# A streaming-encoder layer in one kernel: score offsets by rounded products, merged columns one chunk later, the last expert in halves, one unit of transfers in the columns' buffer

## The reference, cut to what matters

```python
h = rmsnorm(x, g_mix)
proj = h @ w_in                     # q, k, v, pool, z, xbc, dt, three gates of 1024
# differential attention, 4 heads, per head two maps m of 64 columns, causal by blocks of 64
s = einsum('bqhmd,bkhmd->bhmqk', qblk, k)
s = s + bias[None, :, None]         # bias = rel_table[rel_bucket(kpos - qpos)], by head
p = softmax(where(visible, s, -inf))
attn = p[:, :, 0] - lam * p[:, :, 1]
o_a = rmsnorm(attn @ v, subln_g)
o_b = pool_mixer(...); o_c = ssd_mixer(...)
merged = sum_b sigmoid(gate_b) * (o_b @ w_branch[b])
x = x + merged @ w_mix_out
x = x + cross_attention(rmsnorm(x), rmsnorm(mem))      # 4 heads, 256 memory rows
h = rmsnorm(x, g_moe)                                   # router: best group, its best 2 of 4 experts
for e in range(16):
    y = y + comb[:, e:e+1] * ((silu(h @ w_gate[e]) * (h @ w_up[e])) @ w_down[e])
out = rmsnorm(x + y, g_final)
```

## Time and profile before

| | |
|---|---|
| median of 3 runs | 513.97 us (513.95 to 514.27) |
| the profiled execution | 513.97 us |
| its span on the core | 512.2 us |
| TensorE busy | 492.1 us, 96% |
| VectorE busy | 247.9 us, 48% |
| ScalarE busy | 195.6 us, 38% |
| GpSimd busy | 15.7 us, 3% |
| transfers | 149.28 MB, mean 291 GB/s |
| mean granted clock of TensorE | 0.992 |

### The profile page before, as it was taken

The page is one execution under the profiler, slowest core; times in us unless marked ns, Lnnn a source line. Parts: engine busy times, 40 slices in busy tenths (PEclk is TensorE's granted clock), DMA queues, the critical chain, the costliest instruction groups (busy, mean ns, idle before and its releaser), DMA issues.

```text
span 512.2 us, 7124 instructions
## 1 busy us (share of the span) xinstructions
PE 492.1 (96%) x2772; PEld 333.9 (65%) x2772; DVE 247.9 (48%) x469; ACT 195.6 (38%) x349; POOL 15.7 (3%) x30
## 2 busy tenths in 40 slices
PE   7999999999999999999999899999999999999982
PEld 7998998778888988788998534433443344433330
DVE  3764599876788689985664621111111111111113
ACT  5454757446726455445674201111211121111113
POOL 2000100000030000000100000000000000000000
PEclk9999999999999999999999899999999999999998
DMA  7797647643544548896769999999999999999992
GB/s 252 260 312 200 216 132 226 194 117 119 160 162 153 197 125 279 277 355 199 268 230 371 405 401 394 400 399 402 404 402 399 401 400 404 404 399 399 400 357 87
DMA packets 68026, 149.28 MB, mean 291 GB/s; under 512 B 8790, under 2 KB 15124, under 8 KB 67988
## 3 DMA queue, kind: packets, MB, share of 16 engines
q1 hardware_dynamic: 67684, 148.24, 80.5%
q10 hardware_dynamic: 304, 0.53, 0.3%
HBM read 147.69 MB, written 1.05 MB: 290 GB/s over the span
## 4 chain that ended last, share of the span: by engine, by line
issue 47%; PE 34%; DVE 14%; ACT 2%; DMA 1%; POOL 0%; SPq 0%; POOLq 0%; DVEq 0%; ACTq 0%
PE bank L1422 9%; PE bank L1424 9%; PE bank L1423 9%; DVE wl L930 6%; DMA raw<-in_w_in 1%; DVE gates L1189 1%; DVE xc L946 1%; ACT wh L570 1%; PE bank L1445 1%; PE bank L1532 1%; DVE gates L1192 1%; PE bank L1555 1%; DVE big L976 1%; DVE al L916 1%; DVE al L923 1%
## 5 line engine op out<-in xcount | busy, mean ns | idle before, releaser
L930 DVE TENSOR_TENSOR wl<-raw,wh 128x1024 fp32r<-128x1024 f32 (+1 forms) x80 | 94.2, 1195 | 35.2 <-ACT wh L570 33.7
L570 ACT ACTIVATE wh<-raw 128x1024 fp32r<-128x1024 f32 (+1 forms) x80 | 81.9, 1043 | 67.5 <-PE bank L1424 50.8
L1422 PE MATMUL bank<-wh,ah 128*128 128x512 f32 (+2 forms) x248 | 95.0, 383 | 0.0
L1423 PE MATMUL bank<-wl,ah 128*128 128x512 f32 (+2 forms) x248 | 93.3, 376 | 0.0
L1424 PE MATMUL bank<-wh,al 128*128 128x512 f32 (+2 forms) x248 | 93.3, 376 | 0.0
L1424 PEld LDWEIGHTS bank<-wh,al 128*128 128x128 f32 x248 | 46.6, 188 | 8.6
L1422 PEld LDWEIGHTS bank<-wh,ah 128*128 128x128 f32 x248 | 46.7, 188 | 8.3 <-issue 0.3
L1423 PEld LDWEIGHTS bank<-wl,ah 128*128 128x128 f32 x248 | 46.7, 188 | 7.8
L1422 PE MATMUL bank<-ah,wh 128*128 128x256 f32 x160 | 45.8, 286 | 2.2 <-DVE al L916 1.2
L1423 PE MATMUL bank<-al,wh 128*128 128x256 f32 x160 | 45.3, 283 | 0.0
L1424 PE MATMUL bank<-ah,wl 128*128 128x256 f32 x160 | 45.2, 283 | 0.0
(11 more groups left out here) (352 smaller groups left out, 900.1 us busy)
## 6 DMA issues: line engine op xcount, KB each, us to landing
raw<-in_w_in SPq DMA_DIRECT2D x48, 512.0 KB, 4.7
wh_raw<-in_w_exp_up SPq DMA_DIRECT2D x14, 512.0 KB, 12.4
wl_raw<-in_w_exp_gate SPq DMA_DIRECT2D x13, 512.0 KB, 11.2
gates<-in_w_exp_down SPq DMA_DIRECT2D x13, 512.0 KB, 13.3
raw<-in_w_branch SPq DMA_DIRECT2D x12, 512.0 KB, 4.1
ah_raw<-in_w_exp_up SPq DMA_DIRECT2D x10, 512.0 KB, 12.2
al_raw<-in_w_exp_gate SPq DMA_DIRECT2D x10, 512.0 KB, 11.4
gates<-in_w_exp_gate SPq DMA_DIRECT2D x9, 512.0 KB, 11.5
```

The source lines that it names most:

```text
L570: act.activation(dst, src, ACT.Copy, scale=scale).then_inc(done, 1)
L930: dve.tensor_tensor(wl[:, n % RING, 0:sz], raw[:, n % RING, 0:sz], wh[:, n % RING, 0:sz].bitcast(F32), ALU.subtract)\
L1422: pe.matmul(dst, st[0], mv[0], start=start, stop=False, skip_group_check=True)
L1423: pe.matmul(dst, st[0], mv[1], start=False, stop=False, skip_group_check=True)
```

## The change

Six edits stand in one diff.

*Offsets.* The table `toep` is split once into two rounded parts, `bias_hi` (ScalarE, at `n` = `FIRST["bcd"] + 1`, which is behind the cast of chunk 16) and `bias_lo` (VectorE, one `n` later), both [128, 4, 384]: the 256 columns of the second block of queries and again the 128 of the first. The mirror matrix is copied once to the rounded type, `flip_r`. `scores` adds the offsets with four rounded products of 384 columns instead of four float32 ones of 256 and 128. GpSimd's memset of the table's corner comes earlier in its program. The three buffers lie over parts of `gates`.

*Slots.* In slot `s`, `scores(s)` comes ahead of `attn_T(s-1)`.

*Merged columns.* The halves of `to_cols("mix")` come at `LAST["b21"]` and `FIRST["m0"]` instead of `FIRST["b21"]` and `LAST["mka"]`.

*Mean.* The squares are scaled by `D ** -0.5`, and one VectorE instruction makes the mean with its epsilon instead of two.

*Router.* Eleven dummy products ahead of the ranks instead of three; VectorE makes the second half of the gathered rows after `select(0)`; the first gather does the products with the high parts first.

*Last expert and one unit.* The unit of expert 2 that holds the fourth pair of gate and up chunks (`SOLO`) is loaded once into the buffer of the merged columns, `al0`, outside the ring; the other units close up. The last expert's down product, its scaling, subtraction and scatter are done in two halves of 256 columns each, in banks of their own.

```diff
-FILLS = [len(range(s, PASS, RAWX // 2)) for s in range(RAWX // 2)]
+SOLO = UNIT["gu", 2, 3]
+ORDER = [u for u in range(PASS) if u != SOLO]
+FILLS = [len(range(s, len(ORDER), RAWX // 2)) for s in range(RAWX // 2)]
...
-WARM = (10, 6, 5, 6, 0, 0, 4, 3)
+WARM = (10, 6, 5, 6, 0, 0, 4, 11)
...
+        bias_hi, bias_lo = (over_("gates", f"bias_{part}", [P, HEADS, 384], F32R, skip=4 * at)
+                            for part, at in (("hi", 3 * 512), ("lo", 3 * D + 2 * 512)))
+        flip_r = over_("gates", "flip_r", [P, P], F32R, skip=4 * (3 * 512 - P))
...
+        al0_raw = over_("al0", "al0_raw", [P, 2, CH])
+        SOLO_AT = next(j for j, (_, freed) in enumerate(HOMES) if freed == "logits")
+        SOLO_SLOT = len(HOMES) // 2
+        HOMES += [(al0_raw[:, j, :], "values") for j in range(2)]
         FIN_SLOT = RAWG
         g_fin = HOMES[FIN_SLOT][0]
         def fast_fill(u):
-            return u % (RAWX // 2), u // (RAWX // 2) + 1
+            if u == SOLO:
+                return SOLO_SLOT, 1
+            at = ORDER.index(u)
+            return at % (RAWX // 2), at // (RAWX // 2) + 1
+        def landed(slot, times):
+            if slot == SOLO_SLOT:
+                return arrived[0], 16 * len(range(0, CHUNKS, RAW)) + 32
...
-            for c in range(EARLY, 2 * PASS):
-                slot = c % RAWX
-                if c < RAWX:
+            chunks = [2 * u + j for u in ORDER for j in range(2)]
+            for at in range(EARLY, len(chunks)):
+                c, slot = chunks[at], at % RAWX
+                if at == SOLO_AT:
+                    sp.wait_ge(used, LAST["mv"] + 1)
+                    for j in range(2):
+                        load_chunk(2 * SOLO_SLOT + j, 2 * SOLO + j, UNITS)
+                if at < RAWX:
                     free_by = HOMES[slot][1]
                     if free_by == "mixed":
                         sp.wait_ge(s_("cols_pe"), COLS["mix"] + 4)
...
+            g.wait_ge(s_("toep_in"), 16 * HEADS)
+            g.memset(toep[64:P, :, S - SEEN:S], LOW).then_inc(s_("toep_ready"), 1)
             for t in range(T):
                 norm_rstd("mem", t, mem_rs, mem_ss)
-            g.wait_ge(s_("rstd"), NORM["mem"] + T)
-            g.wait_ge(s_("toep_in"), 16 * HEADS)
-            g.memset(toep[64:P, :, S - SEEN:S], LOW).then_inc(s_("toep_ready"), 1)
...
+                if n == FIRST["bcd"] + 1:
+                    act.wait_ge(s_("consts_set"), 1)
+                    act.activation(flip_r[:, :], flip[:, :], ACT.Copy).then_inc(s_("toep_ready"), 1)
+                    act.wait_ge(s_("toep_ready"), 2)
+                    hi_of(bias_hi[:, :, 0:256], toep[:, :, :], s_("toep_ready"))
+                    hi_of(bias_hi[:, :, 256:384], toep[:, :, P:S], s_("toep_ready"))
...
+            def y_last_hi():
+                for j, c in enumerate(COL_HALF):
+                    if j:
+                        act.wait_ge(spent, PASS)
+                    else:
+                        act.wait_ge(filled, len(NAMES) + 1)
+                    act.activation(yh_last[:, c], y_last_bank[j][:, 0:256], ACT.Copy, scale=combs[:, 1:2]).then_inc(s_("y_hi"), 1)
...
-                link(dve.tensor_tensor(ss, ss4[:, 0:2], ss4[:, 2:4], ALU.add))
-                dve.tensor_scalar(ss, ss, 1.0 / D, EPS, ALU.mult, ALU.add).then_inc(s_("x_mean_square"), 1)
+                dve.scalar_tensor_tensor(out=ss, in0=ss4[:, 0:2], scalar=EPS, in1=ss4[:, 2:4], op0=ALU.add, op1=ALU.add)\
+                    .then_inc(s_("x_mean_square"), 1)
...
+                if n == FIRST["bcd"] + 2:
+                    dve.wait_ge(s_("toep_ready"), 4)
+                    for at, lo in ((0, 0), (256, P)):
+                        dve.tensor_tensor(bias_lo[:, :, at:at + S - lo], toep[:, :, lo:S], bias_hi[:, :, at:at + S - lo].bitcast(F32),
+                                          ALU.subtract).then_inc(s_("toep_ready"), 1)
...
-            for t in range(T):
-                moe_rows(t, 0, D // 2)
+            moe_rows(0, 0, D // 2)
...
             link(dve.tensor_tensor(key[:, :, :], bank[1][:, 0:T * EXPERTS].rearrange("p (t n) -> p t n", t=T), chosen, ALU.mult))
             select(0)
+            moe_rows(1, 0, D // 2)
             dve.tensor_copy(totals, bank[1][:, T * EXPERTS:(T + 1) * EXPERTS]).then_inc(s_("totals_ready"), 1)
...
-                    last = n == EXPERTS + 1
-                    y_lo(yl_last if last else yl, yh_last if last else yh, p, ybank(n - 2), n - 1)
+                if 2 <= n <= EXPERTS:
+                    y_lo(yl[:, :], yh[:, :], p, bank[1][:, :], n - 1)
+                if n == EXPERTS + 1:
+                    for j, c in enumerate(COL_HALF):
+                        y_lo(yl_last[:, c], yh_last[:, c], p, y_last_bank[j][:, 0:256], EXPERTS + j)
             with dve.If(over > 0):
...
                     pe.wait_ge(s_("score_exp"), 4 * h)
-                blocks = [(t, w, lo, m, dst[:, 256 * (1 - t):256 * (1 - t) + w])
-                          for t, w, lo in ((1, 256, 0), (0, 128, 128)) for m, dst in enumerate((pS1, pS0))]
-                for t, w, _, m, d in blocks:
+                blocks = [(t, w, m, dst[:, 256 * (1 - t):256 * (1 - t) + w])
+                          for t, w in ((1, 256), (0, 128)) for m, dst in enumerate((pS1, pS0))]
+                for t, w, m, d in blocks:
                     pe.matmul(d, qT[QK * m:QK * m + QK, h, P * t:P * t + P], kT[QK * m:QK * m + QK, h, 0:w],
                               start=(t == 1), stop=False, skip_group_check=True)
-                for t, w, lo, _, d in blocks:
-                    mm = pe.matmul(d, flip[:, :], toep[:, h, lo:lo + w], start=False, stop=True, skip_group_check=True)
+                for dst in (pS1, pS0):
+                    for part in (bias_hi, bias_lo):
+                        mm = pe.matmul(dst[:, 0:384], flip_r[:, :], part[:, h, :], start=False, stop=part is bias_lo, skip_group_check=True)
                 mm.then_inc(s_("scores_pe"), 1)
...
                 if s == 0:
-                    pe.wait_ge(s_("toep_ready"), 1)
...
                         for half in range(2):
                             pe.wait_ge(free[2 * (NAMES.index(nm) % 2) + half], NAMES.index(nm) // 2 + 1)
                 if 2 <= s < 6:
                     attn_o(s - 2)
+                if 0 <= s < 4:
+                    scores(s)
                 if 1 <= s < 5:
                     attn_T(s - 1)
-                if 0 <= s < 4:
...
                     to_cols("mem", hm, s_("mem_rows"), 2, KD, (pS1, pS0, pT, pO), 2)
-                if n in (FIRST["b21"], LAST["mka"]):
-                    half = int(n == LAST["mka"])
+                if n in (LAST["b21"], FIRST["m0"]):
...
+            keep_warm(WARM[7], bank[2])
...
-            pe.wait_ge(s_("sel_ready"), 1)
-            pe.wait_ge(s_("moe_rows"), T)
-            gather(0, 0, bank[3])
+            def down_last(j, fill):
+                slot, times = fill
+                pe.wait_ge(*landed(slot, times))
+                w = [HOMES[2 * slot + i][0].rearrange("p (k n) -> p k n", k=2) for i in range(2)]
+                for c, dst in zip(COL_HALF, y_last_bank):
+                    for kk in range(2):
+                        kt = 2 * j + kk
+                        for i in range(2):
+                            mm = pe.matmul(dst[row_half[i], 0:256], aT[:, kt, row_half[i]], w[i][:, kk, c], start=(kt == 0), stop=(kt == 3),
+                                           skip_group_check=True)
+                    if j and c is COL_HALF[0]:
+                        mm.then_inc(filled, 1)
+                mm.then_inc(spent, 1)
+            def scatter_last():
+                for j, c in enumerate(COL_HALF):
+                    pe.wait_ge(s_("y_lo"), EXPERTS + j)
+                    for t in range(T):
+                        for part in (yh_last, yl_last):
+                            mm = pe.matmul(bank[5 + 2 * t][:, c], selT[:, 1, t, :], part[:, c], start=False, stop=True, skip_group_check=True)
+                        if j:
+                            mm.then_inc(s_("scatter_pe"), 1)
+            def first_gather():
+                pe.wait_ge(s_("sel_ready"), 1)
+                pe.wait_ge(s_("rows_hi"), T)
+                for rows in (rows_hi, rows_lo):
+                    if rows is rows_lo:
+                        pe.wait_ge(s_("moe_rows"), T)
+                    for t in range(T):
+                        for kt in range(2):
+                            mm = pe.matmul(bank[3][:, 256 * kt:256 * kt + 256], rows[:, t, 0:256].rearrange("a (p k) -> a k p", k=2)[:, kt, :],
+                                           sel[:, 0, t, :], start=(rows is rows_hi and t == 0 and kt == 0), stop=(rows is rows_lo and t == T - 1),
+                                           skip_group_check=True)
+                mm.then_inc(s_("gather_pe"), 1)
...
-                    scatter(k // 2, k % 2, (yh_last, yl_last) if k == EXPERTS - 1 else (yh, yl))
+                    scatter(k // 2, k % 2)
```

(7 more changed lines are left out.)

54 lines of the change are left out of this document (29 added, 25 removed).

## The result

The changed kernel takes 515.16 us in the median of 9 runs (514.53 to 516.39), the kernel before 513.97 in 9 runs (513.49 to 515.31). The ratio is 1.0021, 95% interval 1.0012 to 1.0031. The interval leaves 1 out, so the change costs about 1.1 us; that is the very edge of what I had called distinguishable from no change (0.2%). The forecast was 514.2, the range 512.3 to 515.7. Of the four cases the number of the third (515.3) came out, though not by its mechanism.

A forecast was written before the change was run, and what follows sets the result against it. Bounds, stage by stage: the ScalarE-VectorE-TensorE hand-over without slack, VectorE in the slots, TensorE to 183 us, transfers from 290 to 480, then a serial tail. 513.97 + 2.7 − 1.4 − 0.2 − 0.86 = 514.2 us; range 512.3 to 515.7.

The forecast's parts named there:

- the third: The case of Rival 3: slower by the preparation itself or the `x` slots' pause, 515.3 us; chance 0.15.
- Preparation: Rounding the offsets on ScalarE and VectorE makes chunk `pool` 1 start late: +2.7 us, bounds 1.2 and 3.8.
- none of the three hand-overs above has slack: Around 50 to 68 us ScalarE, VectorE and TensorE pass the delay on in full, so `pool` 1 starts 2.7 us late.
- Slots: Attention slots: VectorE is the slower engine; earlier scores remove its 0.72 us wait, plus 0.7 at the last transpose: -1.4 us.
- Merged columns: Products one chunk later: the 0.82 us wait at 216.91 goes, TensorE waits ahead of `m0` until 223.5: -0.2 us, bounds 0 and -0.82.
- Transfers: Ranks, first gather, extra unit: first expert 0.5 us earlier, but transfers bound what follows: 0, up to +1.1 if not covered.
- Tail: Last expert in halves and merged mean, behind the last landing: -0.86 us, bounds -0.4 and -1.4.
- Rival 1: The offsets' preparation is hidden in idle time: 512.2 us taken, 512.7 with 1.2 us left, 511.5 with nothing; chance 0.2.
- Rival 2: TensorE's clock falls behind waits near 71 and 131 us, costing 1.7 us of work: 515.9 us; chance 0.1.
- its dear half: The clock fall of Rival 2 near 131 us, behind the last attention transpose, where nothing hides the 1.7 us.
- Rival 3: Preparation costs 3.8 instead of 2.7 us (four-block accesses half again as dear), or the `x` slots' pause: 515.3 us; chance 0.15.

The follow-up runs named there:

- experiment 1: The changed kernel without the rounded offsets: no preparation on ScalarE and VectorE, float32 offset products of before, all else kept; 513.43 us, ratio 0.9981 to the kernel before.
- experiment 7: The changed kernel with the same offsets prepared earlier, at `LAST["v"]`: ScalarE two chunks earlier, VectorE three; 512.72 us, ratio 0.9967 to the kernel before.
- experiment 2: The changed kernel with the roundings and subtractions of the offsets on GpSimd instead of ScalarE and VectorE; 513.97 us, ratio 0.9993 to the kernel before.
- experiment 12: Early offsets, merged-column products at their old places, no dummies ahead of the ranks, no unit in the columns' buffer (old transfer order); 511.74 us, ratio 0.9955.
- experiment 10: The kernel with the early offsets (experiment 7), without dummy products ahead of the ranks; 512.18 us, ratio 0.9962 to the kernel before.
- experiment 3: The changed kernel with three dummy products ahead of the ranks instead of eleven; 514.67 us, ratio 1.0004 to the kernel before.
- experiment 4: The changed kernel with 22 dummy products ahead of the ranks instead of eleven; 515.89 us, ratio 1.0042 to the kernel before.
- experiment 9: The kernel with the early offsets (experiment 7), with TensorE's products for the merged columns at their old places, one chunk earlier; 512.19 us, ratio 0.9958.

## Why the prediction came out as it did

The time fell into the range, and part of that was luck. Four lines of the ledger came out dearer than forecast (columns 0.30, transfers 0.52, up to the first store 0.41, the stores 0.43), 1.7 us together, and they alone would have given 515.9, above the range. The preparation was cheaper by 0.41 and the program started 0.35 earlier, which took 0.8 back.

**Preparation (+2.7; +2.29 in the trace).** The mechanism was right and is shown from both sides: experiment 1 takes the work away and experiment 7 moves it to idle time, and both bring `pool` 1 back to 56.0 us behind the first product. Up to the start of `dt_arg`'s exponential the arithmetic holds to a hundredth: 57.45 for 55.10 is 2.35 late, 2.70 without the early start of 0.35. The 0.4 that are missing at `pool` 1 are the part of the step that failed, "none of the three hand-overs above has slack": the cast of chunk 19, which follows, is only 2.44 late and that of chunk 20 2.33, so ScalarE had small gaps that my three rows didn't show. In the kernel before it is idle for 0.17 us ahead of chunk 19's cast, in the changed one not at all.

**Slots (-1.4; -1.39).** The sum was right, a reading under it was not. I had VectorE at work "without a gap, except for the 0.72". It also stands idle for 1.79 us in each of the four slots, waiting for ScalarE's exponentials, before (first two rows) and in the changed kernel (third):

```profile
101.26 0.18 DVE L1001 RECIPROCAL small<-small 128x4 f32<-128x4 f32 x1 [1.79 <-ACT pr L616]
110.19 0.18 DVE L1001 RECIPROCAL small<-small 128x4 f32<-128x4 f32 x1 [1.79 <-ACT pr L616]
...
112.14 0.18 DVE L1040 RECIPROCAL small<-small 128x4 f32<-128x4 f32 x1 [1.79 <-ACT pr L639]
```

So VectorE and ScalarE together, each waiting for the other in turn, set the pace of the slots. That TensorE does not is shown by the 1.3 us of low clock, which experiments 2 and 7 don't have and which make no difference at chunk 40. The wait for ScalarE's `ant` copy that I had named is there too, 1.02 us at 112.54. The split was not in the forecast: the two edits overlap (1.13 and 0.84 alone).

**Merged columns (-0.2; +0.10).** The wait that I had foreseen is there, and is longer:

```profile
224.25 0.47 PE L1467 MATMUL bank<-wh,ah 128*128 128x512 f32 x1 [1.12 <-DVEq L1234]
...
223.25 0.69 DVE L1233 SCALAR_TENSOR_TENSOR gates<-gates,bank 128x512 f32<-128x512 f32 x1
...
227.08 1.03 PE L1490 MATMUL bank<-ident,gates 128*128 128x128 f32 x8
```

I had the bank free at 223.5. TensorE started 0.75 later, of which 0.58 is what the whole trace is late there. VectorE's instruction ends at 223.94, which without these 0.58 is the 223.36 of my three rows. The step that failed is the guess of 0.1 for the hand-over to TensorE: it takes 0.31. So the move gains nothing, outside the bounds that I had given.

**Transfers (0; +0.52).** This is the term that failed by most. "The same bytes go over the queue" is true, and the share of 1.04 has not moved. Yet the last landing is later in every trace with the unit in the columns' buffer, and not without it (experiment 12). It does not need the `x` slots' longer pause, for which I had named a price of up to 1.1 (experiment 10). The other half of this term failed too: the first expert was to start 0.5 us earlier, and starts 15.67 us behind chunk 79 instead of 14.38, since the dummies cost more and gave no clock back. As I had it, the transfers hide that. The streams run level for most of the way: the landings 158 and 159 of 192 lie at 178.6 us behind chunk 79 (on average of the two) before and 178.4 changed, the landings 164 and 165 at 186.5 and 187.0, with 400 GB/s moved in both all the while. Counted in bytes they stay level to the end: by 220 us behind chunk 79 all transfers had moved 147.13 MB before, 147.15 changed and 147.06 in experiment 12. So it is not the amount moved that is late, but the completion of single transfers. What shifts it by half a microsecond at the same rate stays open; experiment 12 is one trace, and ties it to the order of the queue, not to a mechanism.

**Tail (-0.86; -0.45).** From the last unit's first product to the third square it is 3.64 us where I had 3.72 and the earlier trace rows gave 4.40. Two things took half of it back. The last unit starts 0.71 us behind its landing instead of 0.31, because the scatter of expert 14, which stands ahead of it, ended only then (its last product starts at 500.94); and the mean saved 0.09 of its 0.18:

```profile
501.26 0.43 PE L1888 MATMUL bank<-x,pr 128*64 128x256 f32 x1
...
503.75 0.60 ACT L902 ACTIVATE hm<-bank 128x512 f32<-128x512 f32 x1
504.90 0.60 ACT L902 ACTIVATE hm<-bank 128x512 f32<-128x512 f32 x1
505.48 0.60 ACT L902 ACTIVATE hm<-bank 128x512 f32<-128x512 f32 x1
...
504.54 1.89 DVE L1448 TENSOR_TENSOR hm<-bank,raw 128x512 f32<-128x512 f32 x3 [0.29 <-ACT hm L902]
506.35 0.15 DVE L948 SCALAR_TENSOR_TENSOR small<-small 128x2 f32<-128x2 f32 x1
```

ScalarE now does all four squares behind the two scalings; before, two of them lay in its wait. VectorE's gain products pile up behind them, and the mean starts at 506.35, when three of them are through. Whether the stores then give the 0.45 back (5.31 on average behind halves, 4.72 behind whole columns, with a scatter of 0.5) is not settled.

**The rivals.** Rival 1, the hidden preparation, did not happen where the change put it, and is what experiment 7 made: its ratio on 513.97 gives 512.3, where I had given 512.2 to 512.7. Rival 2: the clock fell behind the wait of 2.51 us at `pool` 1, to 0.71 over 71 to 75, and the slots' pace hid it. The Trainium skill ("TensorE: Matmul & The Clock Gate", section "HAM oscillation — how this bites in real kernels") says that a long enough wait for data sends the engine back to the lower clock. This trace agrees, and experiment 2, with a wait of 1.01 us at the same place, stays at 1.00. Ahead of the last transposes TensorE waited 0.26 us, not 1, and the clock there stayed at 1.00, so its dear half did not come. The dummies ahead of the ranks did not keep the clock, which is 0.93 over 266 to 290 as before: it fell ahead of them. Rival 3: the preparation in its four-block shape cost what the plain shapes cost (1.58 and 1.82 us), not half again as much; its 515.3 is near the result for other reasons.

## What to carry to other kernels

Work that is added to an engine costs what the hand-over behind it has no slack for, whatever the engine's share says: follow the chunks in flight from engine to engine and look for the place where each has idle time behind its own instruction. The same three roundings and two subtractions cost 2.3 us at one `n` and nothing two to three chunks earlier. An engine that shows idle time can still set the pace, when it and another wait for each other in turn, as VectorE and ScalarE do in the slots. Two edits that take away the same wait don't add up, so test each alone before both are kept.

When the transfers bound the end, compare when the last one lands, not how busy the queue is.

## What the runs showed of the hardware that I had not expected

GpSimd's subtraction and VectorE's did not run side by side: VectorE's took 2.20 instead of 0.71 us and 2.32 instead of 1.23 beside GpSimd's, and 1.21 behind them (experiment 2).

The granted clock of TensorE also fell where the engine had not waited. In the changed kernel it is busy in 4.00 of 4.00 us in the stretches 268 to 272, 272 to 276 and 276 to 280, each at 1.00; then six rows of float32 products with 512 columns take 4.52 us instead of the 2.82 of the first trace before:

```profile
280.81 4.52 PE L1779 MATMUL bank<-x,ident 128*128 128x512 f32 x6
285.17 2.62 PE L1474 MATMUL bank<-ident 128*128 128x128 f32 x22
```

What ran just before were 32 rows of products with 20 columns, with four 128x128 transposes among them. It is so, at 4.34 to 5.47 us, in nine of the fourteen traces, the second one of the kernel before among them, while the first had its fall behind the wait of 1.29 us at 284.25. In the other four (experiments 2, 3, 4 and 9) the clock stays at 1.00 there, though the same products run. The dummies come behind it and neither cause nor prevent it: it falls with none and with eleven, and stays with 3, 11 and 22. What decides is open.
